# A state-space layer inside a float32 two-block model: input stacked by transfers, a fourth readout buffer, two blocks multiplied ahead, the gated output begun before the last readout, and the parameter arithmetic in finer steps

## The reference

```
def sqrelu_mlp(h, w1, w2):                 # w1 2048x8192, w2 8192x2048
    a = relu(h @ w1); return (a * a) @ w2

def s5_mixer(h, a_re, a_im, log_dt, b_re, b_im, c_re, c_im, d_skip, w_glu):
    dt = exp(log_dt)[:, None]; mag = exp(a_re * dt)
    ab = mag * (cos(a_im * dt), sin(a_im * dt))      # 128 groups x 64 states, complex
    coef = (ab - 1) / (a_re, a_im)                   # complex quotient
    bb = coef * b                                    # per group 64 x 16
    u = h.reshape(1, 256, 128, 16)
    bu = einsum('sgc,gpc->sgp', u, bb)
    x = associative_scan(x_t = ab * x_{t-1} + bu_t)  # over the 256 tokens
    y = real(einsum('sgp,gcp->sgc', x, c)) + d_skip * h
    val, gate = split(gelu(y) @ w_glu)               # w_glu 2048x4096
    return val * sigmoid(gate)

h = rmsnorm(x, norm_mix[1]); x = x + s5_mixer(h, ...)
x = x + sqrelu_mlp(rmsnorm(x, norm_mlp[1]), w1[1], w2[1]); return rmsnorm(x, norm_final)
```

## Time and profile before

| | us |
|---|---|
| median of three runs | 3036.42 |
| the profiled execution's own time | 3032.53 |
| its span, first to last instruction | 3030.7 |
| PE busy | 2927.0 (97%) |
| PEld busy | 2662.4 (88%) |
| DVE busy | 1881.2 (62%) |
| ACT busy | 1455.4 (48%) |
| POOL busy | 390.8 (13%) |

### The profile page before, as it was taken

One profiled execution on the slowest core, in us unless ns is written; L12 is line 12 of the kernel. 1 busy time (PEld: TensorE's weight loads), 2 busy tenths in 40 slices (PEclk: granted clock), 3 DMA queues, 4 the chain that ended last, 5 costly groups with the idle time before them and its releaser, 6 DMA issues.

```text
span 3030.7 us, 45330 instructions
## 1 busy us (share of the span) xinstructions
PE 2927.0 (97%) x19056; PEld 2662.4 (88%) x19056; DVE 1881.2 (62%) x2604; ACT 1455.4 (48%) x1996; POOL 390.8 (13%) x444
## 2 busy tenths in 40 slices
PE   8999899999999999999999999989999999999998
PEld 8998888997789998899999999878788999999996
DVE  5997565765455556686656566667555555555555
ACT  5335554545455555444444446447544444444443
POOL 0000000000000000048646651024000000000000
PEclk9999999999999999999999999999999999999999
DMA  6555355441555554567766665633555555555553
GB/s 231 173 189 181 112 195 172 162 139 42 199 179 168 174 168 169 172 220 240 230 216 224 228 225 181 225 116 119 194 182 184 194 191 191 185 194 194 185 191 125
DMA packets 266570, 550.05 MB, mean 181 GB/s; under 512 B 9152, under 2 KB 13376, under 8 KB 266112
## 3 DMA queue, kind: packets, MB, share of 16 engines
q1 hardware_dynamic: 260192, 522.88, 51.8%
q0 software_dynamic: 5456, 21.73, 1.8%
q10 hardware_dynamic: 720, 2.55, 0.2%
HBM read 526.15 MB, written 20.97 MB: 181 GB/s over the span
## 4 chain that ended last, share of the span: by engine, by line
PE 81%; DVE 10%; ACT 4%; DMA 2%; issue 2%; SPq 0%; ACTq 0%; POOL 0%; DVEq 0%
PE G L476 77%; DVE WL L1511 4%; PE T L476 4%; DMA RD<-s_r 2%; DVE Y L1519 2%; ACT WH L977 1%; ACT US L974 1%; PE T L526 0%; DVE TC L1511 0%; DVE US L2121 0%; DMA RAW<-in_even_w_in 0%; DVE ST L1586 0%; ACT T L980 0%; DVE X L1519 0%; ACT Z L980 0%
## 5 line engine op out<-in xcount | busy, mean ns | idle before, releaser
L1511 DVE TENSOR_TENSOR WL<-RAW,WH 128x1024 fp32r<-128x1024 f32 (+1 forms) x948 | 1178.2, 1251 | 824.0 <-ACT WH L977 813.1
L977 ACT ACTIVATE WH<-RAW 128x1024 fp32r<-128x1024 f32 (+1 forms) x948 | 992.6, 1055 | 1078.6 <-PE G L476 1069.7
L476 PE MATMUL G<-A1h,WH 128*128 128x256 f32 x2560 | 725.3, 283 | 7.9 <-DVE WL L1511 7.7
L476 PE MATMUL G<-A1l,WH 128*128 128x256 f32 x2560 | 718.2, 281 | 0.0
L476 PE MATMUL G<-A1h,WL 128*128 128x256 f32 x2560 | 717.9, 280 | 0.0
L476 PEld LDWEIGHTS G<-A1h,WH 128*128 128x128 f32 x2560 | 487.6, 190 | 10.4 <-DVE WL L1511 8.7
L476 PEld LDWEIGHTS G<-A1h,WL 128*128 128x128 f32 x2560 | 488.3, 191 | 0.0
L476 PEld LDWEIGHTS G<-A1l,WH 128*128 128x128 f32 x2560 | 486.6, 190 | 0.8
L476 PE MATMUL G<-WH,Bh 128*128 128x512 f32 x1024 | 399.3, 390 | 0.8 <-DVE WL L1511 0.8
L476 PE MATMUL G<-WH,Bl 128*128 128x512 f32 x1024 | 398.5, 389 | 0.0
L476 PE MATMUL G<-WL,Bh 128*128 128x512 f32 x1024 | 398.4, 389 | 0.0
(11 more groups left out here) (314 smaller groups left out, 3652.0 us busy)
## 6 DMA issues: line engine op xcount, KB each, us to landing
RAW<-in_mlp_w SPq DMA_DIRECT2D x256, 1024.0 KB, 5.4
RAW<-in_even_w_in SPq DMA_DIRECT2D x56, 1024.0 KB, 5.1
RAW<-in_a_w_in SPq DMA_DIRECT2D x48, 1024.0 KB, 5.1
RAW<-in_b_w_glu SPq DMA_DIRECT2D x32, 1024.0 KB, 5.3
RAW<-in_odd_w_in SPq DMA_DIRECT2D x20, 1024.0 KB, 5.0
RAW<-in_even_w_out SPq DMA_DIRECT2D x16, 1024.0 KB, 5.1
RAW<-in_odd_w_out SPq DMA_DIRECT2D x16, 1024.0 KB, 5.1
RAW<-in_a_w_out SPq DMA_DIRECT2D x16, 1024.0 KB, 5.0
```

Source lines behind the costliest of these rows:

```text
L476: return e.matmul(out, lhsT, rhs, start=start, stop=stop, skip_group_check=True)
L977: return e.activation(out, in_, ACT.Copy, scale=scale, bias=0.0)
L1511: return e.tensor_tensor(out, a, b, op)
```

## The change

All parts serve the same stretch and come together:

- Input: the 64 copies into US (48 on DVE, 16 on ACT) become 64 transfers issued by SP, each 32 partitions by 4 rows of 64 numbers; SP issues the last sixteen ahead of `matrices(2)`, which loads block 2.
- Buffers: a fourth RD buffer. WW goes away (DVE writes into XX), XS goes away (POOL writes into ZZ), one of the two WT buffers lies in LAM and the other in the last place of WH.
- Blocks ahead: `within(0)` and `within(1)` run on PE right behind the last down strip, into the free banks G0 and G1, and `turn_w(1)` before the loop. ACT does the root of the norm and the copies of block 0 ahead of the last four HT copies.
- Gated output: `gl` and `gg` swap their pair of banks with what stood before. ACT splits two halves of `gl0` behind block 13's copies, DVE behind the chains 14 and 15; PE multiplies those two halves between `readout(14)` and `readout(15)`.
- Parameters: six empty steps, then one piece at every half, in smaller pieces; the sine moves on ACT from half 10 to half 22, `C_STEPS` and `T_STEPS` later. POOL prepares `masked(0)` between the driving matrices.

```diff
@@ memory
-    WT = [sb(f"WT{i}", [128, 2, 4, 128], ctx=ctx) for i in range(2)]
-    WW = [sb(f"WW{i}", [128, 2, 256], ctx=ctx) for i in range(2)]
+    sb("pad_wt", [128, (RS - 1) * 1024], ctx=ctx)
+    WT = [sb("WT1", [128, 2, 4, 128], ctx=ctx)]
...
+    WT = [LAM[:, :, :, :].rearrange(...)] + WT
-    RD = [sb(f"RD{i}", [128, 2, 4, 160], ctx=ctx) for i in range(2)] + RD
+    RD = [sb(f"RD{i}", [128, 2, 4, 160], ctx=ctx) for i in range(2)] + RD + [sb("RD3", [128, 2, 4, 160], ctx=ctx)]
-    XS = [sb(f"XS{i}", [128, 2, 4, 64], ctx=ctx) for i in range(2)]
@@ the order of strips
     mlp_weights(0)
+    next(turn)
@@ pe
-    C_STEPS = (92, 115, 138, 161)
-    T_STEPS = (200, 201, 202, 203)
+    C_STEPS = (96, 132, 156, 180)
+    T_STEPS = (219, 220, 221, 222)
+    def block_bank(a):
+        return G[a] if a < 2 else TB[2 + a % 2]
...
+        def first_blocks():
+            within(0)
+            within(1)
+        beside(turn_c())
+        mlp(0, A1h, A1l, "s", first_blocks)
         turn_w(0)
-        within(0)
         rows("s", TB[1])
-        for a in range(17):
+        turn_w(1)
+        for a in range(16):
             drive(a)
-            if a < 15:
+            if 1 <= a < 15:
                 turn_w(a + 1)
             feed(a)
-            if a < 15:
+            if 1 <= a < 15:
                 within(a + 1)
             if a:
                 readout(a - 1)
...
-            gemm(f"gl{i}", A1h, A1l, ...)
+            gemm(f"gl{i}", A1h, A1l, ...,
+                 None if i else (lambda: readout(15)))
@@ act
-                if n == 10:
+                if n == 22:
                     e.wait_ge(*d_step["fq"])
                     fn(aw[4], aw[3], ACT.Sin)
                     fn(aw[5], aw[3], ACT.Sin, 0.5).then_inc(*a_step.up("sin"))
...
+        def first_matrices():
+            root(NS[:, 10:12], NS[:, 8:10], "s")
+            turned(0)
+            within(0)
...
-            if a < 8:
-                stack_last(a // 2, 2 * (a % 2))
-                stack_last(a // 2, 2 * (a % 2) + 1)
+            if a == 12:
+                limit[0] = first_half("gl0") + 2
+                for _ in range(2):
+                    split_next()
...
         limit[0] = len(halves)
         e.wait_ge(*fd_mm[15])
-        for _ in range(RS):
+        for _ in range(RS - 2):
             split_next()
         for m in range(4):
             gelus(3, m)
@@ dve
-        beside(every_other())
-        mlp(0, "s", None, None, None, stacks)
+        def params():
+            for _ in range(6):
+                yield
+            yield from s5_params()
+        beside(params())
+        mlp(0, "s", None, None, None, lambda b: ())
...
+            if a in (14, 15):
+                limit[0] = first_half("gl0") + 2
+                split_next()
             if a == 16:
                 limit[0] = len(halves)
-                for _ in range(RS):
+                for _ in range(RS - 2):
                     split_next()
@@ sp
-            if a >= 3:
-                e.wait_ge(*y_mm[a - 3])
+            if a >= 4:
+                e.wait_ge(*y_mm[a - 4])
+        def stacks(b):
+            e.wait_ge(*n_h["s", 2 * b + 1])
+            for m in range(4):
+                for j in range(4):
+                    e.dma_start(stacked(b, m, j), by_phase(b, m, j)).then_inc(*stack[b].up((m, j), 16))
         for c in range(2, len(chunks)):
             if c == first_chunk["gl0"]:
-                for a in range(2):
-                    matrices(a)
+                matrices(0)
+                matrices(1)
+                stacks(0)
+                stacks(1)
+            if c == first_chunk["gl0"] + 1:
+                stacks(2)
+            if c == first_chunk["gl0"] + 2:
+                stacks(3)
+                for a in range(2, 6):
+                    matrices(a)
...
             load(c)
```

More of the change, by code:

```diff
@@ L220, in build_program @@
     HPI = NS[:, 20:21]
+    WT = [LAM[:, :, :, :].rearrange("p a b c -> p (a b c)").rearrange("p (a b c) -> p a b c", a=2, b=4)] + WT
     SPW = nc.dram_tensor("s5_w", (16, 128, 2, 4, 128), F32, kind="Internal").ap()
@@ L397, in build_program @@
     w_back = [sig(f"w_back{i}") for i in range(2)]
-    r_back = [sig(f"r_back{i}") for i in range(3)]
-    stack = sig("stack")
-    stack3 = sig("stack3")
+    r_back = [sig(f"r_back{i}") for i in range(4)]
+    stack = [sig(f"stack{i}") for i in range(4)]
     u_sc = sig("u_sc")
@@ L850, in pe, with mlp @@
         finish()
-        def mlp(l, Ah, Al, ph):
+        def mlp(l, Ah, Al, ph, last=None):
             Bh, Bl = MLP[l][0:2]
@@ L865, in mlp @@
                             beside(norm_block(ph, i, f"m{l}d7{i}"))
+            if last is not None:
+                last()
             finish()
@@ L1021, in squares, with norm_block @@
                        NS[:, 4 * i + blk:4 * i + blk + 1]).then_inc(*n_sq.up((ph, blk, i)))
-        def norm_block(ph, blk, tag, Ah, gains):
+        def norm_block(ph, blk, tag, Ah, gains, between=None):
             squares(ph, blk, x_ready(tag))
             yield
+            if between is not None:
+                between()
             if Ah is not None:
@@ L1346, in act, with mlp @@
         root(NS[:, 10:12], NS[:, 8:10], "m0")
-        def mlp(l, ph, Ah, gains):
+        def mlp(l, ph, Ah, gains, last=None):
             Bh, Bl, RE, SQ = MLP[l]
@@ L1369, in mlp @@
                         if s == 8:
-                            beside(norm_block(ph, i, f"m{l}d7{i}", Ah, gains))
+                            beside(norm_block(ph, i, f"m{l}d7{i}", Ah, gains, last if i == 3 else None))
             finish()
-            root(NS[:, 10:12], NS[:, 8:10], ph)
+            if last is None:
+                root(NS[:, 10:12], NS[:, 8:10], ph)
         def params():
             for n in range(T_STEPS[3] + 1):
-                if n == 10:
+                if n == 22:
                     e.wait_ge(*d_step["fq"])
@@ L2262, in sums, with masked @@
             return d
+        def masked(q):
+            for i in range(2):
+                e.wait_ge(*raw_c[i]["c"])
+                v = BR[i].rearrange("p (a b) -> p a b", b=64)[:, 4 * q:4 * q + 4, :]
+                for g in range(2):
+                    d = e.tensor_scalar(CDQ[i][:, :, 64 * g:64 * g + 64], v, PARITY[:, g:g + 1], 1.0 - 2 * i,
+                                        ALU.mult, ALU.mult)
+            d.then_inc(*p_gen.up(("cd", q)))
         e.memset(STW, 0.0).then_inc(*zeros.up("st"))
@@ L2282, in pool @@
                 e.memset(STR, 0.0).then_inc(*zeros.up("str"))
[L2284 removed]
+            if a == 4:
+                e.wait_ge(*c_par["c"])
+                masked(0)
         e.wait_ge(*zeros["str"])
[L2287 to L2296 removed]
         for a in range(16):
@@ L2386, in matrices @@
             e.wait_ge(*sp_r[a])
-            e.dma_start(RD[a % 3][:, :, :, :], SPR[a]).then_inc(*r_back[a % 3].up(a, 16))
+            e.dma_start(RD[a % 4][:, :, :, :], SPR[a]).then_inc(*r_back[a % 4].up(a, 16))
+        def stacks(b):
[3 more added lines that the diff above has]
+                    e.dma_start(stacked(b, m, j), by_phase(b, m, j)).then_inc(*stack[b].up((m, j), 16))
         for c in range(2, len(chunks)):
             if c == first_chunk["gl0"]:
-                for a in range(2):
+                matrices(0)
[8 more added lines that the diff above has]
+                    matrices(a)
+            if c == first_chunk["gl0"] + 3:
+                for a in range(6, 10):
                     matrices(a)
             if c == first_chunk["gg0"]:
-                for a in range(2, 16):
+                for a in range(10, 16):
                     matrices(a)
```

101 lines of the change are left out of this document (38 added, 63 removed).

## The result

The changed kernel takes 3050.39 us (median of 6 runs, 3044.38 to 3055.27), the kernel before 3034.23 us (6 runs, 3030.56 to 3039.16). The ratio is 1.0054, 95% interval 1.0038 to 1.0069, or some 16 us. The forecast was 3031.6, with a range of 3018 to 3042, so it was wrong in sign and the time lies outside the range. The two profiled executions show the same difference: 3049.15 against 3032.53 us, spans of 3047.3 and 3030.7.

The account below looks back on a forecast made before the run. PE, busy 97% of the span, was taken as the bound, leaving only idle or slowed time. Terms -7.4 + 6.8 - 0.9 + 1.3 - 7.7 + 3.1 = -4.8 gave 3027.7 profiled, 3031.6 as median; range 3018 to 3042.

Parts of the forecast that it names:

- The head: Start of the blocks: PE stands 8.6 us for WB(2), drive(2) at E+28.9 against E+27.6, +1.3 us.
- HT at E+10.2: Head of the blocks: ACT's HT copies complete 10.2 us after E, the end of the last down strip.
- sixteen take 6.7: Head: SP issues the last sixteen stacking transfers about 0.42 us apart, 6.7 us, with WB(2) behind them.
- a spacing far from 0.42: Sign that the prediction is wrong: SP's issues at the head spaced far from 0.42 us.
- The sine: First MLP: PE idles 5.1 us for the sine's chain, plus 1.7 us of slow clock, +6.8 together.
- the blocks: Drive(2) to drive(15): RD issued one block earlier shortens each block from 7.90 to 7.30 us, -7.7.
- the low parts of the parameters: First MLP: five PE waits for DVE's low parts, 5.8 us, and 1.6 us of slow clock go, -7.4.
- the tail up to half 4: From drive(15) (D) to half 4 of gl0: half 4 starts at D+30.9 instead of D+29.5, +1.4 us.
- The last row of the table: Half 4 of gl0 to the end: slow clock behind PE's 9 us wait, forecast +1.7, measured +3.8.
- The slower rival: Head: short runs hold the DMA engines, up to +27 us (3058), deciding from 0.73 us per transfer; chance 0.19.
- the prediction's other case: Head: if runs below 512 B are read, modified and written, WB(2) lands later, as in the slower rival.

Follow-up runs that it names:

- e1: Changed kernel with the old order of the RESCALE steps: 3037.76 us, ratio 1.0017 to the kernel before.
- e2: Kernel before with only the new order of the RESCALE steps: 3042.72 us against 3032.04, ratio 1.0038.
- e10: e7 plus halves 4 and 5 of gl0 split ahead of the last GELUs: 3005.16 us, ratio 0.9906 to the kernel before.
- e7: Changed kernel with old RESCALE, stacking transfers interleaved with block matrices in SP's queue, sine at half 18 instead of 22: 3009.00 us, ratio 0.9917 to the kernel before.
- e5: Kernel before with the new RESCALE order and one empty step behind its first: 3034.12 us against 3034.19, ratio 0.9996.
- e9: e7 with readout(15) put ahead of gl0 again: 3006.11 us, ratio 0.9909 to the kernel before.
- e11: e9 with ACT splitting halves 4 and 5 of gl0 between the last GELUs: 3006.68 us, ratio 0.9911 to the kernel before.

## Why the prediction was wrong

- **A part left out.** The description ahead says that all parts serve the same stretch, and the prediction has no term outside it. `RESCALE` acts 400 us earlier, is used by PE, ACT and DVE, and costs 8.7 us in the profile and some 11 by the times of e1 and e2. No mechanism was misjudged here; the line was not weighed. The order of DVE and ACT in `aq0` would have shown the update and its squares in one half. This alone turns the forecast of -4.8 into a loss.
- **The head, mis-sized.** Its steps were right up to HT at E+10.2, and the stall came where it was named. The term "sixteen take 6.7" was taken at 0.42 us from transfers out of memory; the runs show 0.68, and the prediction had named a spacing far from 0.42 as a sign of being wrong. And only the last sixteen were summed: the price applies to the 48 ahead as well, which begin at 1969.5 and so end 5.4 us after HT is ready. 5.4, 3.6 more for the last sixteen, and 2.0 more of slow clock behind the longer wait (0.50 from the wait's end to 2025), less 1.2 for a quicker landing (3.6 against 4.8), make 9.8 of the 9.9 missing at drive(2).
- **The sine, the blocks, the low parts of the parameters, the tail up to half 4** came within 1 us each. In the tail there was some luck: readout(14) began at D+4.8, not D+4.4, but the clock fell later than summed and it took 2.45 us, not 3.5. In e10, where the clock fell at once, it took 3.68 and the GELUs start at D+17.3. One reading was wrong at no cost: before, DVE did mostly one piece of small operations, of 4 to 14, behind every second split, not two between two splits. e7, with the sine level, gains 8.4 us from 1210 to 1925, beside the -7.4 forecast for the parameter waits.
- **The last row of the table** has 1.6 us for the slow clock behind the 9.1 us wait, as forecast (1.7); of the other 2.2, 1.6 come in one piece near 2317. Both kernels wait 2.8 us for X there; behind it the clock is at 0.50 and 0.67 for 4 us in the changed kernel and at 1.00 in the kernel before, but also at 0.61 and 0.53 in e5, which has all of the kernel before at this place. So it comes and goes from execution to execution, and the change isn't needed for it.
- **The slower rival** named short runs and a bound of 0.73 us per issue. The right queue and nearly the right spacing, but the wrong mechanism: the transfers land in 1.9 us (median), the DMA engines aren't held, and its bound was too high, since it too counted only sixteen. The Trainium skill (DMA: Bandwidth & Descriptors, Why small descriptors are slow (HBM only)) says that transfers from SBUF to SBUF do not suffer from short runs. The landings of 1.9 us don't speak against it, though no run has such a transfer with long runs to compare; the prediction's other case, that WB(2) lands later behind them, did not come (3.6 us, where 4.8 was summed). What the stacking costs is the issue of its 64 transfers.

The change was worth having: with the old table, another queue order, the sine four halves earlier and two early splits (e10) it is 0.94% faster than before (0.80 to 1.07%), 29 us, and the faults had eaten all of it and more.

## What to carry to other kernels

List every edited table with the engines and the stretch that read it before pricing any part; a reordered table of steps is priced by which steps fall into the same slot on two engines that feed each other. When copies become transfers, price the queue as a whole: number of transfers times the spacing, from the first moment it may start, against the time at which the first load behind them is needed. Where one engine's wait moves by n slots, move what it waits for by the same n.

## What was not expected of the hardware

- An issue from SP of a transfer of 32 partitions by 4 or 8 rows of 256 bytes costs 0.68 to 0.70 us of its queue on average (the instruction itself 0.60), against 0.32 for the instruction of RD's 640 KB; twice the bytes and runs change it by 0.02.
- Two idle times of 1.7 us, each with a readout of sixteen small products behind it, went with a granted clock of 0.50 for 14 us in e9 and e11, while one idle time of 1.7 us, a readout and 24 products of `gl0` went with 3 to 7 us (in the changed kernel 0.50, 0.66, then 1.00 from 2132).
